# A hybrid attention block on one core: equal score pieces, a reworked head front, stage boundary and gate round trips

## The reference

```python
h = rmsnorm(x, g_norm_mix)
proj = h @ w_in                                       # 1024 x 5168, split among the branches
# index scores of a query against every key; the best 256 keys of each query are kept
rel = relu(einsum('bqhd,bsd->bqhs', qi_b, k_idx))     # 8 index heads of width 32
score = einsum('bqhs,bqh->bqs', rel, wi_b) * idx_scale
score = where(visible, score, NEG_INF)                # block-causal
top_val, top_idx = top_k(score, 256)
# mLSTM gates: running sums and maxima over chunks of the sequence
b = cumsum(log_sigmoid(f_pre)); m_new = maximum(b_last + m_st, max(b_last - b + ig))
```

## Time and profile before

| | |
|---|---|
| three runs | 3425.85, 3427.1, 3435.36 us; median 3427.1 |
| profiled execution | 3430.0 us, of which the span of its instructions is 3428.1 |
| PE busy | 3001.6 us (88%) |
| DVE busy | 2487.1 us (73%) |
| ACT busy | 1815.9 us (53%) |
| POOL busy | 448.2 us (13%) |
| mean granted TensorE clock | 0.943 of full speed |
| head, tail, attention begin at | 0, 357.2, 1209.5 us |

### The profile page before, as it was taken

How to read it: one execution, slowest core, us unless ns; L and a number is a source line. 1 busy time by engine, 2 the same in 40 slices (tenths; PEclk the granted TensorE clock), 3 DMA queues, 4 the chain that set the end, 5 groups by cost and what they waited for, 6 DMA issues and landing times. The chain is left out here.

```text
span 3428.1 us, 45107 instructions
## 1 busy us (share of the span) xinstructions
PE 3001.6 (88%) x12983; PEld 2229.5 (65%) x12984; DVE 2487.1 (73%) x3909; ACT 1815.9 (53%) x2523; POOL 448.2 (13%) x597
## 2 busy tenths in 40 slices
PE   6998699899999967888899689999499999999980
PEld 5766478578678734444455367787388888888870
DVE  5477588789989956666663344442799999999984
ACT  5322467577578434343334333332377777777760
POOL 0211110100000042211111000000111111111113
PEclk9999899999999979999999899999699999999995
DMA  3222322222222274444323466552578879667878
GB/s 123 79 76 65 106 83 71 64 70 74 69 68 74 68 173 115 115 101 113 79 80 68 100 203 171 167 172 92 196 275 306 325 281 352 249 241 271 310 277 349
DMA packets 368639, 537.52 MB, mean 157 GB/s; under 512 B 36704, under 2 KB 201856, under 8 KB 368368
## 3 DMA queue, kind: packets, MB, share of 16 engines
q1 hardware_dynamic: 337936, 426.51, 40.3%
q0 software_dynamic: 28256, 100.85, 7.8%
q10 hardware_dynamic: 2304, 8.39, 0.6%
HBM read 510.70 MB, written 129.80 MB: 187 GB/s over the span
## 5 line engine op out<-in xcount | busy, mean ns | idle before, releaser
L908 DVE TENSOR_TENSOR e_w_lo<-e_raw,e_w_hi 128x1024 fp32r<-128x1024 f32 x386 | 447.0, 1220 | 4.3 <-ACT e_w_hi L770 4.3
L1560 PE MATMUL x_ps<-h_hi,x_w_hi 128*128 128x512 f32 (+1 forms) x1024 | 401.8, 392 | 0.0
L1560 PE MATMUL x_ps<-h_hi,x_w_lo 128*128 128x512 f32 (+1 forms) x1024 | 400.9, 391 | 0.0
L1560 PE MATMUL x_ps<-h_lo,x_w_hi 128*128 128x512 f32 (+1 forms) x1024 | 400.8, 391 | 0.0
L770 ACT CAST e_w_hi<-e_raw 128x1024 fp32r<-128x1024 f32 x386 | 377.0, 1055 | 5.8 <-PE e_pG L712 5.8
L1750 DVE TENSOR_SCALAR_CACHE_REDUCE x_relu<-x_score,x_cand 128x1024 uint8<-128x1024 f32 (+3 forms) x217 | 315.6, 1487 | 3.6
L1663 ACT ACTIVATE x_relu<-x_score,x_cand 128x896 int8<-128x896 f32 (+3 forms) x217 | 281.0, 1296 | 56.9 <-DVE x_cand L1757 56.6
L2332 DVE CUSTOM_DVE_ANT_0 t_junk<-t_L,t_mask 128x512 bf16<-128x512 f32 (+3 forms) x320 | 185.7, 607 | 166.2 <-PE t_L L2114 165.0
L2304 ACT ACTIVATE t_probT<-t_ST 128x512 f32<-128x512 f32 x272 | 160.8, 593 | 261.7 <-PE t_ST L2145 261.1
L2153 PE MATMUL t_O<-t_probT,t_v 128*65 128x512 f32 x544 | 289.5, 614 | 10.6 <-ACT t_probT L2304 8.7
L712 PE MATMUL e_pG<-e_w_hi,e_x_hi 128*128 128x512 f32 x768 | 246.8, 403 | 3.6 <-DVE e_x_lo L903 3.6
(11 more groups left out here) (406 smaller groups left out, 6209.9 us busy)
## 6 DMA issues: line engine op xcount, KB each, us to landing
e_raw<-in_w_exp_gate SPq DMA_DIRECT2D x392, 256.0 KB
e_raw<-in_w_exp_up SPq DMA_DIRECT2D x392, 256.0 KB
e_raw<-in_w_exp_down SPq DMA_DIRECT2D x192, 512.0 KB
projT<-x_out SPq DMA_DIRECT2D x124, 256.0 KB
slot_out<-e_y POOLq DMA_DIRECT2D x48, 512.0 KB, 6.6
o_gate<-projT SPq DMA_DIRECT2D x32, 512.0 KB
x_w_raw<-in_w_in SPq DMA_DIRECT2D x31, 512.0 KB
a_tables<-in_x SPq DMA_DIRECT2D x16, 512.0 KB, 4.7
```

The source lines that it names most:

```text
L908: nc.vector.tensor_tensor(w_lo[:, u, :], raw[:, u, :], w_hi[:, u, :].bitcast(F32), ALU.subtract).then_inc(gl, 1)
L1560: last = nc.tensor.matmul(ps[0:w, u % 4, :], wt[:, m % 2, kk, 0:w], ht[:, kk, q * 512:(q + 1) * 512], start=(kk == 0 and s == 0), stop=(kk ...
```

## The change

Four edits.

1. `pieces(n)` cuts a block's width into as few pieces of at most 1024 as before, but of equal width up to 128: 640 and 512 for block 8, 640 and 640 for 9, 768 and 640 for 10, 768 and 768 for 11, 896 and 768 for 12, 896 and 896 for 13. Blocks up to 7, and 14 and 15, are cut as before.
2. The head's front: the gain is loaded third and the first weights after four token tiles; ScalarE loads its square root table first, does one square between two tiles' copies and a root for every two tiles; VectorE starts with the tokens and reckons the angles behind them; TensorE puts a unit's steps ahead of a tile's transposes; the sines come last.
3. The boundary between head and tail: the head makes a tenth tile (9, plain, stored from `X`), and loads, converts and splits the first two tiles of the tail, whose weight buffers now live across both stages. The tail has 31 tiles; TensorE makes 16 parts (`AT_ONCE`) ahead of the first scores, and the pace spreads the others.
4. The gates: six small loads go from SP's queue to GpSimd's, ahead of its setup, and the read of each round trip comes two to four steps behind its write, with the users moved back as well.

```diff
-ORDER = (6, 7, 8, 4, 0, 1, 2, 3, 5)
+ORDER = (6, 7, 8, 4, 0, 1, 2, 3, 5, 9)
 HEAD = len(ORDER)
+READY = 2
 HUNITS = HEAD * NCH
 TAIL = CT - HEAD
 UNITS = TAIL * NCH
-IDX, KEY, ROPED = 8, 12, 32
...
         def load(m):
+            tile = ORDER[m] if m < HEAD else m
             sp.wait_ge(wl_ok, m)
-            sp.dma_start(w_raw[:, :, :], w_v[:, :, ORDER[m] * P:(ORDER[m] + 1) * P]).then_inc(w_in, 16)
+            sp.dma_start(w_raw[:, :, :], w_v[:, :, tile * P:(tile + 1) * P]).then_inc(w_in, 16)
...
-        for t in range(4):
+        for t in range(2):
+            tokens(t)
+        sp.dma_start(gain, i["g_norm_mix"].partition_broadcast(P)).then_inc(consts, 16)
+        for t in range(2, 4):
+            tokens(t)
+        sp.dma_start(w_raw[:, :, :], w_v[:, :, ORDER[0] * P:(ORDER[0] + 1) * P]).then_inc(w_in, 16)
+        for t in range(4, XT):
             tokens(t)
...
-        sp.dma_start(gain, i["g_norm_mix"].partition_broadcast(P)).then_inc(consts, 16)
-        sp.dma_start(w_raw[:, :, :], w_v[:, :, ORDER[0] * P:(ORDER[0] + 1) * P]).then_inc(w_in, 16)
-        for t in range(4, XT):
-            tokens(t)
...
-            if IDX <= u < KEY:
+            if IDX <= u < KEY or PLAIN <= u < HUNITS:
+                tile = ORDER[u // NCH]
                 sp.wait_ge(x_ok, u + 1)
-                sp.dma_start(proj[8 * P:9 * P, cols(u % NCH)], X[:, u % 3, :]).then_inc(x_st[u % NCH], 16)
-            if u >= 3:
+                sp.dma_start(proj[tile * P:(tile + 1) * P, cols(u % NCH)], X[:, u % 3, :]).then_inc(x_st[u % NCH], 16)
+            if 3 <= u < PLAIN + 3:
                 store(u - 3)
-            if u % NCH == 2 and u // NCH + 2 < HEAD:
+            if u % NCH == 2 and u // NCH + 2 < HEAD + READY:
                 load(u // NCH + 2)
...
-        pe.wait_ge(ident_ok, 3)
+        pe.wait_ge(ident_ok, 2)
         for t in range(NT):
-            turned(t)
             if t >= 4:
                 unit(t // 4 - 1, 2 * (t % 4), 2 * (t % 4) + 2)
+            turned(t)
         for u in range(NCH - 1, HUNITS + LAG):
             if u < HUNITS:
                 unit(u)
@@ -1189,7 +1191,7 @@
                 tables(0)
             if u == FILL + 2:
                 tables(8)
-            for x in range(u - LAG + 1) if u == FILL else [u - LAG] if u > FILL else []:
+            for x in range(u - LAG + 1) if u == FILL else [u - LAG] if FILL < u < PLAIN + LAG else []:
...
-        squares(0)
+        def square(t):
+            act.wait_ge(x_in[t % XT], 16 * (t // XT + 1))
+            if t:
+                act.wait_ge(sq_done, t)
+            nc.scalar.activation(junk, x_t[:, t % XT, :], ACT.Square, accum_out=ss[:, t:t + 1]).then_inc(sq_done, 1)
+            if t % 2:
+                act.wait_ge(sq_done, t + 1)
+                nc.scalar.activation(rt[:, t - 1:t + 1], ss[:, t - 1:t + 1], ACT.Sqrt, bias=eps[:, :], scale=1.0 / DM).then_inc(rt_done, 1)
+
+        def turned(t):
+            for h, ks in halves(t):
+                act.wait_ge(tr_done, h + 1)
+                nc.scalar.copy(h_hi[:, ks, t * P:(t + 1) * P], aux[:, h % 2, :].rearrange("p (k n) -> p k n", n=P)).then_inc(hi_done, 1)
+        act.wait_ge(eps_ok, 1)
+        nc.scalar.activation(rt[:, 0:1], eps[:, :], ACT.Sqrt).then_inc(table_ok, 1)
+        act.wait_ge(table_ok, 1)
+        for t in range(4):
+            square(t)
         weights(0)
-        squares(1)
-        turned(0)
+        for t in range(NT):
+            turned(t)
+            if t + 4 < NT:
+                square(t + 4)
+            if t in (8, 12):
+                take(t // 4 - 2)
+            if t == 10:
+                weights(1)
+        take(2)
         act.wait_ge(sin_arg, 1)
         nc.scalar.activation(sin[:, :, :], ang[:, :, :], ACT.Sin).then_inc(sin_ok, 1)
         nc.scalar.activation(kh[:, :, :], ang[:, :, :], ACT.Sin, scale=0.5).then_inc(sin_ok, 1)
-        squares(2)
-        turned(1)
-        squares(3)
-        take(0)
-        turned(2)
-        weights(1)
-        take(1)
-        turned(3)
-        take(2)
...
-            if u % NCH == 1 and 2 <= u // NCH + 1 < HEAD:
+            if u % NCH == 1 and 2 <= u // NCH + 1 < HEAD + READY:
...
+        dve.wait_ge(consts, 16)
+        for t in range(NT):
+            if t % 2 == 0:
+                inverse_roots(t // 2)
+            scaled(t)
+            if t:
+                turned(t - 1)
+            if t == 2:
+                weights(0)
+            if t == 12:
+                weights(1)
+        turned(NT - 1)
...
-        dve.wait_ge(consts, 16)
-        for t in range(NT):
-            if t % 4 == 0:
-                squares(t // 4)
-            scaled(t)
-            if t == 0:
-                weights(0)
-            if t:
-                turned(t - 1)
-            if t == 12:
-                weights(1)
-        turned(NT - 1)
...
-        for u in range(ROPED + 3):
+        for u in range(HUNITS + 2):
             if u == FILL + 2:
                 for a in range(8, 16):
                     expand(a)
             if 0 <= u - 3 < ROPED:
                 low(u - 3)
-            if u % NCH == 1 and 2 <= u // NCH + 1 < HEAD:
+            if u % NCH == 1 and 2 <= u // NCH + 1 < HEAD + READY:
...
-    return [(a, min(width(n), a + 1024)) for a in range(0, width(n), 1024)]
+    step = P * -(-(n + 1) // -(-width(n) // 1024))
+    return [(a, min(width(n), a + step)) for a in range(0, width(n), step)]
...
+AT_ONCE = 2 * KT
...
-        self.per = self.total() / (UNITS * KT)
+        self.per = self.total() / (UNITS * KT - AT_ONCE)
...
-        return min(UNITS * KT, int(self.us / self.per))
-
-
-def tail_and_index(pg, h_hi, h_lo):
+        return min(UNITS * KT, AT_ONCE + int(self.us / self.per))
...
-        w_raw = sb("w_raw", [P, KT, P])
-        w_hi, w_lo = sb("w_hi", [P, 2, KT, P], F32R), sb("w_lo", [P, 2, KT, P], F32R)
...
-                if m:
-                    sp.wait_ge(wl_ok, m)
+                if m > READY:
+                    sp.wait_ge(wl_ok, m - READY)
                 sp.dma_start(w_raw[:, :, 0:w], w_v[:, :, at:at + w]).then_inc(w_in, 16)
...
-            load(0)
...
-            load(1)
...
-                    if q == 0:
-                        pe.wait_ge(wl_ok, m + 1)
+                    if q == 0 and m >= READY:
+                        pe.wait_ge(wl_ok, m - READY + 1)
...
+            while done < AT_ONCE:
+                part(done)
+                done += 1
...
-                act.wait_ge(w_in, 16 * m + 16)
-                if m >= 2:
-                    act.wait_ge(unit_ok, NCH * (m - 1))
+                act.wait_ge(w_in, 16 * (m - READY) + 16)
+                act.wait_ge(unit_ok, NCH * (m - 1))
...
-            weights(0)
-            act.wait_ge(wl_ok, 1)
-            weights(1)
-            state[1] = 2
+            state[1] = READY
...
-                dve.wait_ge(wh_ok, m + 1)
+                dve.wait_ge(wh_ok, m - READY + 1)
...
+            state[0] = READY
...
+        g_in, c_in, taps = pg.sw_sem("t_g_in"), pg.sw_sem("t_u_in"), sem("u_taps_ok")
...
-            sp.dma_start(gI[:, :], rows(C_IF)).then_inc(g_in, 16)
-            sp.dma_start(gF[:, :], rows(C_IF + MH)).then_inc(g_in, 16)
-            sp.dma_start(bi[:, :], i["b_igate"]).then_inc(g_in, 16)
-            sp.dma_start(bf[:, :], i["b_fgate"]).then_inc(g_in, 16)
-            sp.dma_start(wt[:, :, :], i["w_conv_mlstm"]).then_inc(c_in, 16)
-            sp.dma_start(bt[:, :], i["b_conv_mlstm"]).then_inc(c_in, 16)
...
                 if f == 4:
                     sp.wait_ge(g_w, 1)
                     sp.dma_start(end_d, ends[:, :]).then_inc(g_dma, 16)
+                if f == 6:
                     sp.wait_ge(g_dma, 16)
...
-                if f == 7:
+                if f == 9:
                     sp.wait_ge(g_w, 2)
                     sp.dma_start(car_d.rearrange("(h c) k -> h c k", c=NT), C2[:, :, :]).then_inc(g_dma, 16)
+                if f == 11:
                     sp.wait_ge(g_dma, 48)
...
-                if f == 14:
+                if f == 17:
                     sp.wait_ge(g_w, 3)
...
+                if f == 20:
...
+            rows = lambda at: pg.d["projT"][at:at + MH, :].rearrange("h (c n) -> (h c) n", n=P)
+            pool.dma_start(gI[:, :], rows(C_IF)).then_inc(g_in, 16)
+            pool.dma_start(gF[:, :], rows(C_IF + MH)).then_inc(g_in, 16)
+            pool.dma_start(bi[:, :], i["b_igate"]).then_inc(g_in, 16)
+            pool.dma_start(bf[:, :], i["b_fgate"]).then_inc(g_in, 16)
+            pool.dma_start(wt[:, :, :], i["w_conv_mlstm"]).then_inc(c_in, 16)
+            pool.dma_start(bt[:, :], i["b_conv_mlstm"]).then_inc(c_in, 16)
...
-                if f == 12:
+                if f == 17:
...
-                if f == 11:
+                if f == 15:
...
-                        act.wait_ge(c_in, 33)
+                        act.wait_ge(taps, 1)
...
-                    v_.tensor_scalar(bt[:, :], bt[:, :], 0.5, None, ALU.mult).then_inc(c_in, 1)
```

(15 more changed lines are left out.)

45 lines of the change are left out of this document (14 added, 31 removed).

## The result

Beside the kernel before on one chip the changed kernel took 3409.8 us (median of five runs, 3409.4 to 3413.3) against 3431.4; the ratio is 0.9937, with an interval of 0.992 to 0.9953. The forecast was 3379.7 us, a ratio of 0.986, with a range of 3356 to 3404. So the sign was right, and the time lies 6 us outside the range. Four later measurements, each against the kernel before measured beside it on the same chip, gave ratios of 0.9914, 0.9915, 0.9926 and 0.9921 (intervals of about 0.0015 on either side): 25 to 30 us. The first is the least of five, and all of them are well short of the 47 us that the sum promised. Three of the four later medians (3397.5, 3396.0 and 3398.8 us) lie inside the stated range, so what failed is the sum more than its upper end.

The account below looks back on a forecast made before the run. No engine bounds it throughout: round trips set the scoring, VectorE and TensorE nearly tie in the searches. Front and boundary -7.4, scores -18, searches -10, gates -12 sum to -47.4, from 3427.1 to 3379.7 us; range 3356 to 3404.

Parts of the forecast that it names:

- The front: Kernel's start, up to the last h_lo subtraction: ends at 62 us instead of 75.0, a gain of 13 (6 to 17).
- The boundary: Between head and tail: tenth tile 23.0 us, stage start 4.2, first score 14.0 later; costs 5.6 us.
- The slower rival: Front, 16 parts and first quad: TensorE stays at 1.2 GHz, +19, +8 and +55 us, total 3462; chance 0.04.
- The scores: Scoring of blocks 8 to 13: equal pieces save 22.6 us, less 4.6 for ScalarE's copies and conversion; booked -18 (-10 to -22).
- The formula of relu, sum and 0.14 us: Scoring heads, relu plus sum plus hand-overs: 1.72 us (blocks 8, 9), 1.98 (10, 11), 2.21 (12, 13) instead of 2.44.
- the rival of the full ScalarE: Scoring: ScalarE's copies or a TensorE part fill the shorter head, so -18 becomes -6, total 3392; chance 0.12.
- some 36 us earlier: Sign in the tail: its last part comes some 36 us earlier against the first score.
- The searches: Tail's binary searches: one tile fewer and 16 parts ahead give 14.7 us by the ledger; booked -10 (-3 to -25).
- The gates: Attention's first steps: write-to-read distance shortens stalls at steps 8, 12 and 20, 17.6 us in all; booked -12 (0 to -20).
- The stall of 12 us ahead of chunk 0 stays: it hangs on loads at step 23: Early attention: the 12 us stall ahead of chunk 0 was taken as unchanged by the gate edit.
- the gate stalls come back: Attention's gate part: the stalls return as waits for the busy DMA engines, total 3391; chance 0.08.
- no SP wait over 2 us at the gate reads: Sign at the attention's gate reads: SP's waits, 5.1, 5.3 and 7.3 us before, all at most 2 us.

Follow-up runs that it names:

- boundary_undone: Changed kernel with the boundary as before (nine tiles in the head, 32 in the tail, no parts at once): 3401.2 us, 3.7 above the changed kernel.
- at_once_none: Changed kernel without the 16 parts ahead of the scores: 3395.1 us, ratio 0.9912 to the kernel before.
- packed rows: Changed kernel with the two gate arrays stored in DRAM as chunk, head, column (a chunk's row 2 KB in one piece): 3358.3 us, ratio 0.9806.
- rows_first: Changed kernel with a chunk's four loads that don't need the convolution's stores issued first, the other two last: 3412.4 us, 7.7 slower than the changed kernel.
- after_again: The changed kernel unaltered, measured again on another chip: 3397.5 us against 3427.0 for the kernel before, ratio 0.9914.

## Why the prediction was wrong, by its own steps

**The front** was right: 11.9 us won (the last h_lo starts at 62.44, predicted about 62), where 13 was booked with a range of 6 to 17. The angle arithmetic stayed under cover as argued: from the end of the front to the end of the ninth tile it is 265.1 us, where before it was 265.3.

**The boundary** cost 7.5 us, not 5.6: one term was mis-sized. The tenth tile took 25.2 us, not 23.0, and a row tells why:

```profile
328.07 0.60 PE L1178 MATMUL a_aux<-a_ident,a_x 128*128 128x128 f32 x4
330.38 0.50 PE L1142 MATMUL a_ps<-h_hi,w_hi 128*128 128x512 f32 x1 [1.71 <-DVE w_lo L1302]
```

Its first unit waits for the split of its own weights, which stands in VectorE's queue behind the rope of the tile before. I had counted the split as added work and not asked what it is queued behind. The other two terms fit: the stage starts 4.4 us behind the last unit (4.2), and the first score comes 13.7 behind that (14.0, though the reason given for it, the 16 parts, was only part of it: without them it was 3.5 us less). The slower rival, TensorE at the lower clock, did not come as a whole: behind an idle stretch of 4.5 us TensorE's matmuls stood 0.43 us apart for the first 2.7 us of the stage, which is the lower level, and 0.23 from there; the granted clock was 0.91 in the boundary and 1.00 in the 78 us behind it. The rule that the prediction cites for it from the Trainium skill (TensorE: Matmul & The Clock Gate, "HAM oscillation") was borne out in the fall of the clock behind the wait, but not in what the rival made of it, that the clock stays down.

**The scores.** The formula of relu, sum and 0.14 us held to 0.02 us: heads take 1.72, 1.96 and 2.20 us (1.72, 1.98, 2.21 predicted). What failed is the deduction. 22.6 less 4.6 were booked and 15.1 came, and of blocks 12 to 15 came 0.4 where their formula gave 3.7. The rows of ScalarE in block 12 show it:

```profile
865.77 0.92 ACT L1643 ACTIVATE x_relu<-x_z 128x896 f32<-128x896 f32 x1 [1.05 <-PE x_z L1584]
866.59 0.58 ACT L1627 COPY x_out<-x_ps 128x512 f32<-128x512 f32 x1
867.05 0.84 ACT L1643 ACTIVATE x_relu<-x_z 128x768 f32<-128x768 f32 x1
868.11 1.73 ACT L1643 ACTIVATE x_relu<-x_z 128x896 f32<-128x896 f32 x2 [0.22 <-PE x_z L1584]
869.74 1.04 ACT L1620 CAST w_hi<-w_raw 128x1024 fp32r<-128x1024 f32 x1
```

Two relus of such a head (0.92 + 0.84) leave 0.4 us of 2.2, a unit's copy needs 0.58 and a conversion 1.04, so heads of this block with one of them took 2.34 to 2.66 us, and one of block 13 took 3.26. That is the rival of the full ScalarE, in part: its chance was 0.12 for the whole, and it took 3 us more than I had allowed. Undoing the pieces showed one more thing that was missing from the step, that some 3 of the 16 us are paid back in the searches. (The sign "some 36 us earlier" did not follow from the sum, which had 28; the last part came 29.5 us earlier against the first score.)

**The searches** came out at -11.0 for a forecast of -10, and this number was better than its working. It rested on the slower pace of 48 parts fewer; boundary_undone and at_once_none show that 32 of them were worth 14 us and the other 16 nothing. (The moved tile also took its four copies, its conversion and its split along; which of these the searches felt was not taken apart.)

**The gates** are the step that failed. The single stalls went as argued (6.7 and 2.6 us at steps 8 and 20, predicted 7.9 and 4.1; step 12's stall stayed, 9.0 us for 7.8). The sentence that failed is "The stall of 12 us ahead of chunk 0 stays: it hangs on loads at step 23". I took it for a fixed length. It is a wait for an arrival: in each of the 15 profiles with unpacked rows (rows_first aside), step 31 starts 4.6 us behind the landing of `WI`, which lands 13.9 to 15.6 us behind its issue. SyncE issued this load 85.3 us after step 0, where before it was 86.5, as its own waits and the convolution's units, loaded and stored over the same queue, stand ahead of it; in the profile after_again it was 81.2. Step 31 came 0.8 and 5.6 us sooner than before, by the same 1.2 and 5.3 us within half a us, whatever steps 0 to 29 had saved (3.5 and 7.0); step 30 waited out the rest. On average the eleven profiles with the new gate part have this issue at 83.0 us and step 31 at 102.3, the four with the old one at 86.3 and 105.5: 3.2 us of the 12, and 1.4 of them are lost ahead of step 0 (30.9 us behind the last mark, 29.6). My rival for this ("the gate stalls come back", 0.08) had the right outcome and the wrong mechanism: not busy DMA engines but two loads served at 40 GB/s. And "no SP wait over 2 us at the gate reads", the sign I named, did not show, because two steps between a write and its read are no distance on a queue that has nothing to do between them (5.8, 2.5 and 6.4 us).

**What was not in the sum** is the 10.1 us of the 240 late steps, and this is not settled. Their length in kernels with unpacked rows and the old gate part was 592.0, 591.6, 590.1 and 591.2 us, and in eleven with the new one (rows_first aside) 590.5 to 602.1, 595.8 on average. Chance alone is an unlikely reading of that (four out of fifteen would lie so low in about 3 cases of 100), but no row shows what the gate part would leave behind for step 75 or 120, and the part on GpSimd's queue is not it (597.1 without). The longer steps are those beside a chunk (75, 90, 105, 120, 135). The length goes with the landing of their row loads: in the five profiles in which the fourth `WI` took 15.5 us or more the late part took 595.0 to 602.1, in the ten others (13.9 to 14.9 us) 590.1 to 597.1. That fits a wait for the rows, but is no proof of it. And with packed rows the late part took 559.6, 560.8, 557.8 and 557.8 us, with and without the gate part, so the spread went with the stall.

Added up for the first profile: 3.0 us from the front and the boundary, 2.9 from the scores, -1.0 from the searches, 1.2 ahead of step 0, 11.2 from the gates, 10.1 from the late steps and -0.6 behind them are the 27 us between -47.4 and -20.7. The range allowed the gates to give nothing; what it had no room for is the 10.1 us of the 240 steps behind, which the prediction held for fixed.

## What to carry to other kernels

A stall that ends with an arrival is not a length but a date: before booking a gain ahead of it, follow the arrival back to the queue that issues it and ask whether that comes sooner. A step's number is a distance only for the engines that the steps pace. And a row of waits behind a DMA deserves a reading of the time from issue to landing beside loads of the same size; here what that showed was worth more than the four edits together (38 us against 22 to 30).

## What was not expected of the hardware

- Two loads that spread rows of 512 bytes from DRAM over 128 partitions moved 39 to 41 GB/s, where loads of the same size and packet length from different addresses moved 277. The first kind went at 70 packets a us, the second at nearly 600. In rows of 2 KB they landed in 5.0 us instead of 10.9 and 15.8.
- The DMA share of such a stretch was 1.01 in one profile and 0.17 in another of the same kernel, at the same rate. Here only the rate could be read.
- With 976 or 992 matmul parts beside the same scores and searches the tail took the same time (798.7 and 798.6 us), with 1024 it took 812.7.
